# Two decoder layers with routed experts: the order of the expert blocks, the choice of experts and the causal mask are rearranged

## The chip, the cores and the metric

The kernel runs on one core of one Trainium2 chip, as one launch. The metric is the device time of one execution in microseconds. The kernel before takes 2188.45 us, the median of three timed runs (2186.95 to 2190.23). All traces show one profiled execution.

## The reference

Two layers over 1024 tokens of width 1024, all in f32. A layer is:

```python
h = h + concat(rmsnorm(SGU), rmsnorm(Conv), rmsnorm(MLA)) @ w_o     # three mixers on rmsnorm(h)
m = rmsnorm(h, ffn_norm_g);  h = h + hier_moe(m, ...)
h = h + sigmoid(rmsnorm(h) @ ple_gate_w) * rmsnorm(p @ ple_proj_w)
```

MLA is causal attention with 8 heads (`s = where(kpos <= qpos, s, -1e30)` before the softmax). What matters here is the expert part:

```python
glog = t @ wg + bg;  g_idx = argmax(glog);  g_w = softmax(glog)[g_idx]      # 4 groups
elog = (t @ we + be) restricted to the 8 experts of group g_idx
topv, topi = top_k(softmax(elog), 2);  topv = topv / sum(topv)
# each of the 2048 (token, choice) pairs goes to its expert; for an expert e and its rows xb:
hb = silu(xb @ w_gate[e]) * (xb @ w_up[e])          # w_gate, w_up: 1024 x 256, w_down: 256 x 1024
out[token] += (hb @ w_down[e]) * g_w * topv
```

Each expert's weights are 3 MB. Its rows are grouped in blocks, and a block needs the expert's weights once.

## The kernel before

Each engine has its own program, and semaphores order them. `Steps` names the steps of one chain: `X.next("name")` is what an instruction signals, `X.after(l, "name")` what another waits for. A layer runs through these stages (times of layer 1 in the profiled execution):

- **Input projection and mixers** (to about 245 us): eight tiles of 128 tokens in a loop.
- **Attention** (245 to 437 us): 8 heads of 8 query tiles, written out. For tile `j` PE computes `scores` (L1942 to L1968): one or two products of 96 rows by up to 1024 columns into PSUM, and then the product of `ident_b` and `mask_b` on the diagonal block (L1967), which adds -1e30 above the diagonal and signals the tile. VectorE takes the maximum (`row_max`, L1458), ScalarE the exponential with that as its bias (L1064), PE transposes it (L1976) and multiplies by the values (L1996). PE issues the scores of the next tile ahead of the transposes of the present one. VectorE also runs the taps of a convolution in between (L1290).
- **Output projection** (437 to 592 us): a loop over tiles. VectorE's and ScalarE's programs are real loops (`lag_loop`, L414), two tiles a turn, in which each stage `(o, fn)` works on tile `t + o`; PE's is written out (L2064). VectorE's order (L1510) is: `norm_m` of the tile before (L1262, the norm whose result goes to the experts), `norm(1)` of tile t+2 (L1253), copy of the transposes of t+1 (L1269), `conv_centre` of t+3, copy of `turn_m` (L1274), the first half of `h +=` (L1503), `conv_scale`, `conv_silu` of t+3 (L1382), the second half, `g_main` (L1508, the router's logits of tile t-1), `conv_out` of t+3 (L1387). The three convolution steps run in iterations 0 to 4 only (tiles 3 to 7; tiles 0 to 2 are done inside attention). PE's order is: first half of the projection, `turn(1)` of t+1, `conv_back`, `turn_m` of t-1, second half, `conv_turn` of t+3 (L1869, needs `conv_silu`), the logits of t-1, `pointwise`. Behind the loop comes tile 7's remainder: `norm_m`, `turn_m`, logits.
- **Router** (592 to 625 us): a chain of small VectorE steps over all tiles (L1531 to L1666), each of which waits for the one before (`link`, L1516). It chooses a group and two experts for each token (L1531 to L1559), `picked` (L1557) goes to PE for the counts (L2093, L2097), which PE issues behind `project(0)` and `project(1)` (L2082), products for the last line of the layer. Then the blocks are laid out. `owner_f`, `owner_i` (L1620, L1621) write each block's expert to `cells`; SP waits for that and loads the weights of blocks 0, 1 and 2 (L650 to L658). The one-hot products (L1630, L1631, L2119, L2122) give the lists of rows (`list_i`, L1662), for which GpSimd waits before it gathers the rows of the first three blocks (L817).
- **Experts** (625 to 957 us): an expert with a remainder of up to 64 rows gets a *small* block (64 rows) for it, all else goes to *full* blocks (128 rows). Blocks come in pairs: the small one first, on even positions, the full one behind it. `n_pairs` is the larger of the number of full blocks and half of all blocks, rounded up, and 2 x `n_pairs` blocks are run (`n_blocks`, L1639). Three buffers `slot` hold weights. For block b PE's order is: gate and up (L2160 full, L2156 small), transposes of the rows of b+1 (L2141), down of b-1 (L2181 full, L2175 small), transposes of the hidden units (L2188). SP loads gate and up of b+2 (L643, L644) when those of b-1 have been used, and down of b+2 (L648) when `down` of b-1 is finished. `block_loop` (L462) unrolls six blocks, with a guard for each step.
- **Last line of the layer** (957 to 1110 us), which starts when all blocks are stored.

## Time and profile before

| | us |
|---|---|
| timed runs, median of 3 | 2188.45 |
| the profiled execution | 2190.6 |
| its span, first to last instruction | 2188.8 |
| PE matmuls busy | 2000.5 (91%) |
| VectorE busy | 1009.4 (46%) |
| ScalarE busy | 638.8 (29%) |
| GpSimd busy | 374.5 (17%) |
| DMA moved 362 MB, mean | 165 GB/s |

The chain of work that ended last is the thread to follow: it starts at the last instruction and steps back to whatever released each one. By engine it is 76% PE, 11% DMA, 5% VectorE, 4% issue, 3% ScalarE. The DMA share lies in the two expert stages. The mean granted TensorE clock was 0.969 of full speed. In the rows, `PE` is a matmul, `PEld` a weight load, `DVE` VectorE, `ACT` ScalarE, `POOL` GpSimd, `SPq` SP's queue; a release is shown as `[idle before <-releaser]`. A matmul on f32 stands as two instructions.

### The profile page before, as it was taken

Reading aid. Unit: us, or ns where it says so; the run is one execution under the profiler, and the core shown is the slowest. Engines: PE = TensorE matmul, PEld = TensorE weight load, DVE = VectorE, ACT = ScalarE, POOL = GpSimd, SP = SyncE. Lnnn points to the kernel's source line nnn. Section 1 sums busy time; section 2 is a strip of 40 time slices with the busy share of each in tenths; the row PEclk is TensorE's granted clock in tenths of the full one; section 3 lists DMA queues with packets and bytes.
Section 4 is the critical chain, followed back from the end, with each engine's and each line's share of the span. In section 5 each row is a group of like instructions: output and inputs, shape, how many; then the busy total and the mean of one; then the engine's idle time right before and its main releaser. Section 6 shows DMA issues by size and latency. Waiting matters only on the chain.

```text
span 2188.8 us, 34749 instructions
## 1 busy us (share of the span) xinstructions
PE 2000.5 (91%) x9032; PEld 1110.8 (51%) x9032; DVE 1009.4 (46%) x2247; ACT 638.8 (29%) x1521; POOL 374.5 (17%) x542
## 2 busy tenths in 40 slices
PE   6999799899969999989979998998999699999898
PEld 3555466655535455544435554666555354445344
DVE  2489756654341111124434897566543421111253
ACT  3333355522111111131133333555221111111221
POOL 2232100021012222210022221000210122221100
PEclk9999899999979999999989998999999799999999
DMA  7011241000389999955210112410004799999422
GB/s 249 15 29 29 59 153 30 25 20 29 140 308 396 380 382 378 389 217 192 88 29 15 29 29 61 152 30 25 20 29 154 292 393 381 377 380 353 175 87 96
DMA packets 122222, 361.98 MB, mean 165 GB/s; under 512 B 18853, under 2 KB 54005, under 8 KB 105220
## 3 DMA queue, kind: packets, MB, share of 16 engines
q1 hardware_dynamic: 105028, 318.74, 40.2%
q0 software_dynamic: 14784, 33.59, 4.1%
q10 hardware_dynamic: 2304, 8.39, 0.9%
q8 instruction: 48, 0.79, 0.1%
q14 instruction: 58, 0.48, 0.1%
HBM read 319.50 MB, written 59.51 MB: 173 GB/s over the span
## 4 chain that ended last, share of the span: by engine, by line
PE 76%; DMA 11%; DVE 5%; issue 4%; ACT 3%; SPq 1%; DVEq 0%; POOL 0%; ACTq 0%; POOLq 0%
PE ps L1801 30%; DMA region_c<-in_moe_w_up_dram 8%; PE ps L2160 7%; PE ps L1964 5%; PE ps L1822 4%; PE ps L2156 4%; PE ps L1996 3%; PE ps L2181 3%; PE ps L1976 3%; PE ps L1770 3%; PE ps L2175 2%; PE ps L2141 2%; PE ps L1896 2%; DMA region_a<-in_moe_w_up_dram 2%; PE ps L2082 2%
## 5 line engine op out<-in xcount | busy, mean ns | idle before, releaser
L1801 PE MATMUL ps<-region_b,region_c 128*128 128x512 f32 x1024 | 451.5, 597 | 7.7 <-DVE region_c L1269 7.7
L1801 PEld LDWEIGHTS ps<-region_b,region_c 128*128 128x128 f32 x1024 | 192.8, 191 | 234.4 <-issue 233.9
L1801 PE MATMUL ps<-region_a,region_c 128*128 128x512 f32 x512 | 225.3, 594 | 0.0
L1680 DVE SCALAR_TENSOR_TENSOR region_a<-region_a,ps 128x128 f32<-128x128 f32 x66 | 23.4, 354 | 387.0 <-ACT region_a L1132 382.7
L2160 PE MATMUL ps<-region_c,region_a 128*128 128x512 f32 x336 | 148.8, 596 | 12.9 <-DMA region_c<-in_moe_w_up_dram 12.8
L1801 PEld LDWEIGHTS ps<-region_a,region_c 128*128 128x128 f32 x512 | 96.9, 191 | 118.0 <-issue 118.0
L1460 DVE TENSOR_REDUCE neg_max<-ps 128x1 f32<-128x128 f32 (+7 forms) x128 | 97.0, 758 | 109.8 <-PE ps L1967 109.0
L1964 PE MATMUL ps<-region_c 96*128 96x512 f32 (+3 forms) x384 | 146.9, 492 | 0.0
L1132 ACT ACTIVATE region_a<-ps 128x128 f32<-128x128 f32 x66 | 21.8, 330 | 364.7 <-PE ps L2160 243.5
L1976 PE MATMUL ps<-ident,region_a 128*128 128x128 f32 x576 | 91.1, 285 | 25.2 <-ACT region_a L1064 25.0
L2160 PEld LDWEIGHTS ps<-region_c,region_a 128*128 128x128 f32 x336 | 62.1, 190 | 92.9 <-issue 92.9
L1822 PE MATMUL ps<-region_a,region_c 128*128 128x416 f32 x256 | 96.2, 530 | 3.7 <-ACT region_c L940 3.0
L1770 PE MATMUL ps<-ident,region_c 128*128 128x128 f32 x496 | 66.7, 281 | 35.9 <-DVE region_c L1253 30.3
L1064 ACT ACTIVATE region_a<-ps,neg_max 128x128 f32<-128x128 f32 (+7 forms) x128 | 96.2, 752 | 0.1
L2156 PE MATMUL ps<-region_c,region_a 128*64 128x256 f32 x736 | 88.7, 395 | 5.4 <-DMA region_c<-in_moe_w_up_dram 4.0
L2160 PE MATMUL ps<-region_a 128*128 128x512 f32 x192 | 85.2, 596 | 6.7 <-DMA region_a<-in_moe_w_up_dram 5.2
L1770 PEld LDWEIGHTS ps<-ident,region_c 128*128 128x128 f32 x496 | 59.2, 144 | 61.8 <-DVE region_c L1253 34.1
L1996 PE MATMUL ps<-region_a,region_c 128*64 128x128 f32 x1152 | 84.0, 278 | 2.4 <-ACT region_a L1052 2.0
L1976 PEld LDWEIGHTS ps<-ident,region_a 128*128 128x128 f32 x576 | 61.5, 140 | 48.5 <-ACT region_a L1064 35.6
L1996 PEld LDWEIGHTS ps<-region_a,region_c 128*64 128x64 f32 x1152 | 68.9, 136 | 26.4 <-issue 26.4
L1964 PEld LDWEIGHTS ps<-region_c 96*128 96x128 f32 x384 | 65.2, 196 | 31.2 <-issue 30.8
L1049 ACT COPY region_a<-ps 128x512 f32<-128x512 f32 (+3 forms) x128 | 64.8, 506 | 55.8 <-PE ps L1976 55.8
(351 smaller groups left out, 3065.4 us busy)
## 6 DMA issues: line engine op xcount, KB each, us to landing
region_c<-in_moe_w_gate_dram SPq DMA_DIRECT2D x44, 1024.0 KB
region_c<-in_moe_w_up_dram SPq DMA_DIRECT2D x44, 1024.0 KB
region_c<-in_moe_w_down_dram SPq DMA_DIRECT2D x44, 1024.0 KB
region_a<-in_moe_w_gate_dram SPq DMA_DIRECT2D x22, 1024.0 KB
region_a<-in_moe_w_up_dram SPq DMA_DIRECT2D x22, 1024.0 KB
region_a<-in_moe_w_down_dram SPq DMA_DIRECT2D x22, 1024.0 KB
region_c<-choice_outputs SPq DMA_DIRECT2D x32, 512.0 KB, 4.4
qk_heads<-gains SPq DMA_DIRECT2D x32, 384.0 KB, 3.9
```

Source lines behind the costliest of these rows:

```text
L1049: ins = nc.scalar.copy(prob_t[j % 2][:, 0:w], bank(4, 0, w * P).rearrange("p (k q) -> p k q", q=P))
L1064: nc.scalar.activation(prob[j % 2][:, 0:n], banks(2 * (j % 2))[:, 0:n], ACT.Exp, bias=neg_max[:, j % 2:j % 2 + 1], accum_out=denom[:, j:j ...
L1460: v.tensor_reduce(neg_max[:, j % 2:j % 2 + 1], banks(2 * (j % 2))[:, 0:(j + 1) * P], AX.X, ALU.max, negate=True).then_inc(*X_max.next(f"ma ...
L1770: ins = T(bank(b + k // 4, P * (k % 4), P * (k % 4) + P), src[:, P * k:P * k + P], ident[:, :])
L1801: ins = mm(dst, lhsT[:, k, :], w[:, k, a:b], start=(k == 0), stop=(k == KD - 1))
L1822: ins = mm(bank(4, 0, MLA_IN), aT_mix[u][:, k, :], w_in[:, k, 1024:IN], start=(k == 0), stop=(k == KD - 1))
L1964: mm(bank(b + c // 512, 0, w), q, k_ring[u][0:QK, c:c + w], start=True, stop=not last, skip_group_check=True)
L1976: ins = T(bank(4 + k // 4, P * (k % 4), P * (k % 4) + P), prob[j % 2][:, P * k:P * k + P], ident[:, :])
L1996: ins = mm(ps[a:a + HEAD, 6, 0:P], vals[:, k, head, :], prob_t[c][:, k, :], start=(k == 0), stop=(k == j + c), tile_position=(0, a), skip_ ...
L2156: ins = mm(ps[a:a + HALF, 2, 0:F].rearrange("p (a f) -> p a f", a=2), xT[:, k, 0:HALF], pair[:, :, P * c:P * c + P], start=(k == 0), stop= ...
L2160: ins = mm(bank(2).rearrange("p (a f) -> p a f", a=2), xT[:, k, :], w_gu[s][:, :, k, :], start=(k == 0), stop=(k == KD - 1))
L2181: ins = mm(bank(4 + half), hid_t[:, k, :], w_dn[s][:, k, 512 * half:512 * half + 512], start=(k == 0), stop=(k == 1))
```

## The change

Four edits, none of which changes what is computed:

1. **Mask.** For tiles `j >= MASKED = 3` PE's mask product is left out, and `row_max` adds `mask_b` to the diagonal block in PSUM before it takes the maximum. VectorE waits for its own addition.
2. **Choice by tile.** `choose(t)` is a new last-but-one stage of VectorE's loop in the output projection, behind `g_main` and ahead of `conv_out`. It has 15 steps, each waiting for the one before, and takes the place of the router's 23 steps over all tiles. The exponential of the groups on ScalarE, `g_sum` and `g_w` move behind.
3. **Owners early.** `owner_f` and the two halves of `owner_i` are moved from behind `fields` to behind `key`.
4. **Full first.** In each pair the full block comes first, the small one second (all the places with `True` and `False` swap, and the lists are written to the other parity). If there are fewer small blocks than pairs, the last position is dropped (`no_last` is -1 or 0). As the numbers of full and small blocks can now differ, `cells` has separate counts of finished ones.

```diff
@@ VectorE, attention
                 def row_max(hh, j):
                     v.wait_ge(*S_pe.after(hh, f"s{j}"))
+                    if j >= MASKED:
+                        own = banks(2 * (j % 2))[:, j * P:(j + 1) * P]
+                        v.tensor_tensor(own, own, mask_b[:, :], ALU.add).then_inc(*X_mask.next(f"mask{j}"))
+                        v.wait_ge(*X_mask.after(hh, f"mask{j}"))
@@ PE, scores
+                    if j >= MASKED:
+                        ins.then_inc(*S_pe.next(f"s{j}"))
+                        return
@@ VectorE, output projection
+                def choose(t, u, i):
+                    g = TILES * l + t
+
+                    def link(ins, name):
+                        ins.then_inc(*CH_vec.next(name))
+                        v.wait_ge(*CH_vec.after(g, name))
+
+                    v.wait_ge(*G_vec.after(g))
+                    g_max, g_first, m1, i1, m2, i2 = (span(sm(k), t, 1) for k in (0, 3, 4, 5, 6, 7))
+                    gl_, el = lg[:, t, 0:NG], lg[:, t, NG:NG + NE]
+                    link(v.tensor_reduce(g_max, gl_, AX.X, ALU.max), "g_max")
+                    link(v.tensor_scalar(g_gap[:, t, :], gl_, g_max, None, ALU.subtract), "g_diff")
+                    link(v.scalar_tensor_tensor(g_cand, gl_, g_max, order[:, 0:NG], ALU.is_lt, ALU.add), "g_cand")
+                    link(v.tensor_reduce(g_first, g_cand, AX.X, ALU.min), "g_first")
+                    link(v.tensor_scalar(g_far, order[:, 0:NG], g_first, -BIG, ALU.not_equal, ALU.mult), "g_far")
+                    link(v.tensor_tensor(e_in.rearrange("p (g e) -> p g e", g=NG), el.rearrange("p (g e) -> p g e", g=NG),
+                                         g_far.unsqueeze(2).to_broadcast([P, NG, EPG]), ALU.add), "e_in")
+
+                    def largest(src, top, where, hot, n):
+                        link(v.tensor_reduce(top, src, AX.X, ALU.max), f"m{n}")
+                        link(v.scalar_tensor_tensor(cand, src, top, order[:, :], ALU.is_lt, ALU.add), f"cand{n}")
+                        link(v.tensor_reduce(where, cand, AX.X, ALU.min), f"i{n}")
+                        v.tensor_scalar(hot, order[:, :], where, None, ALU.is_equal).then_inc(*CH_vec.next(f"hot{n}"))
+
+                    largest(e_in, m1, i1, hot1[:, t, :], 1)
+                    v.wait_ge(*CH_vec.after(g, "hot1"))
+                    link(v.scalar_tensor_tensor(e_rest, hot1[:, t, :], -2 * BIG, e_in, ALU.mult, ALU.add), "rest")
+                    largest(e_rest, m2, i2, hot2[:, t, :], 2)
-                             (3, late(conv_scale)), (3, late(conv_silu)), (0, w_main(1)), (-1, g_main), (3, late(conv_out))])
+                             (3, late(conv_scale)), (3, late(conv_silu)), (0, w_main(1)), (-1, g_main), (-1, choose), (3, late(conv_out))])
@@ VectorE, router (23 steps g_max .. hot2 over all tiles removed)
+                v.wait_ge(*K_pe.after(l, "owners"))
+                link(v.tensor_copy(owner, ps[0:1, 6, 256:256 + POS]), "owner_f")
+                at_place = cells[0:1, 0:POS].rearrange("p (r a) -> p a r", a=2)
+                link(v.tensor_scalar(at_place[:, 0], owner[:, NE:POS], NE - 1, None, ALU.bitwise_and), "owner_full")
+                link(v.tensor_scalar(at_place[:, 1], owner[:, 0:NE], NE - 1, None, ALU.bitwise_and), "owner_i")
...
-                link(v.tensor_scalar(total, n_pairs[0:1], 2.0, None, ALU.mult), "n_blocks")
+                link(v.tensor_scalar(no_last, n_half[0:1], n_pairs[0:1], 1.0, ALU.is_ge, ALU.subtract), "no_last")
+                link(v.scalar_tensor_tensor(total, n_pairs[0:1], 2.0, no_last, ALU.mult, ALU.add), "n_blocks")
...
+                link(v.tensor_tensor(run[:, 4:5], run[:, 4:5], n_pairs[0:1], ALU.add), "run_pairs")
+                small_now = last_rows[0:1, 210:211]
+                link(v.tensor_tensor(small_now, no_last, n_pairs[0:1], ALU.add), "small_now")
+                link(v.tensor_tensor(run[:, 5:6], run[:, 5:6], small_now, ALU.add), "run_small")
@@ PE, experts (the same swap on ScalarE, VectorE and GpSimd)
-                turn_x(prev, 0, 0, True)
-                gate_up(prev, 0, 0, True)
-                turn_x(prev + 1, 1, 0, False)
-                turn_h(prev, True)
+                turn_x(prev, 0, 0, False)
+                gate_up(prev, 0, 0, False)
+                turn_x(prev + 1, 1, 0, True)
+                turn_h(prev, False)
```

## Rows read from the trace of the kernel before

**Rows 1.** Chain that ended last, one mask product in attention: start, us, what.
```profile
359.96 0.06 PE ps L1967
```
**Rows 2.** Windows: length, busy of each engine, granted clock, DMA share, GB/s; both expert stages.
```profile
620.00:940.00 320.00, 297.50 (x1547) 160.23 (x1548) 61.79 (x154) 52.44 (x132) 79.94 (x130) 0.97 1.00 383
1713.00:2022.00 309.00, 281.30 (x1457) 150.38 (x1458) 57.85 (x144) 48.84 (x122) 75.06 (x122) 0.97 0.99 378
```
**Rows 3.** Timeline, tile 6 of a head: start, us, engine, line, op.
```profile
360.06 1.09 DVE L1460 TENSOR_REDUCE neg_max<-ps 128x1 f32<-128x896 f32 x1 [0.28 <-PE ps L1967]
361.25 0.29 DVE L1468 TENSOR_TENSOR region_a<-ps,rden 128x128 f32<-128x128 f32 x1
361.52 1.02 ACT L1064 ACTIVATE region_a<-ps,neg_max 128x896 f32<-128x896 f32 x1
```
**Rows 4.** Two lines alone: duration in ns, min, median, max; first and last start.
```profile
L1322 DVE TENSOR_SCALAR st_c<-st_c x16: 169/170/171, 347.7 to 1614.5; 128x4 f32<-128x4 f32 x16
...
L1407 DVE SCALAR_TENSOR_TENSOR region_b<-region_b,r_c,k_gain x16: 243/246/248, 31.7 to 1302.5; 128x32 f32<-128x32 f32 x16
```
**Rows 5.** Timeline of VectorE, output projection of layer 1.
```profile
512.26 0.20 DVE L1508 TENSOR_TENSOR region_a<-ps,router_b 128x36 f32 x1 [1.25 <-PE ps L1801]
513.19 0.42 DVE L1387 SCALAR_TENSOR_TENSOR region_a<-ps,vecs 128x256 f32 x1 [0.73 <-PE ps L1876]
...
517.93 1.14 DVE L1253 SCALAR_TENSOR_TENSOR region_c<-region_a,rstd,gains 128x256 f32<-128x256 f32 x2
520.82 0.69 DVE L1269 COPY region_c<-ps 128x512 f32<-128x512 f32 x1 [1.74 <-PE ps L1770]
...
526.84 0.43 DVE L1382 SCALAR_TENSOR_TENSOR region_b<-region_b 128x256 f32<-128x256 f32 x1 [0.48 <-ACT region_b L971]
...
566.23 0.20 DVE L1508 TENSOR_TENSOR region_a<-ps,router_b 128x36 f32 x1 [1.02 <-PE ps L1801]
...
582.63 0.20 DVE L1508 TENSOR_TENSOR region_a<-ps,router_b 128x36 f32 x1 [1.03 <-PE ps L1801]
```
**Rows 6.** Timeline of VectorE, router of layer 1: linked steps with fixed addresses.
```profile
609.10 0.42 DVE L1602 SCALAR_TENSOR_TENSOR region_c<-vecs,ps 128x256 f32<-128x256 f32 x1
...
612.87 0.21 DVE L1620 CAST region_c<-ps 1x64 int32<-1x64 f32 x1
613.11 0.18 DVE L1621 TENSOR_SCALAR cells<-region_c 1x64 int32<-1x64 int32 x1
```
**Rows 7.** Timeline of VectorE, a later loop: linked steps that address by tile.
```profile
1015.82 1.28 DVE L1713 SCALAR_TENSOR_TENSOR h<-region_c,moe_weights,h 128x1024 f32 x1
1017.25 1.28 DVE L1716 SCALAR_TENSOR_TENSOR h<-region_c,moe_weights,h 128x1024 f32 x1
```
**Rows 8.** Chain that ended last, output projection and start of the router.
```profile
528.74 0.22 PE ps L1869 x2
...
573.01 0.87 PE ps L1770 x8
...
584.05 2.06 DVE region_c L1262
...
592.52 9.35 PE ps L2082 x16
```
**Rows 9.** Chain that ended last, first gather and first blocks of layer 1.
```profile
625.35 7.84 DMA region_a<-moe_inputs,block_tokens
...
642.12 7.11 PE ps L2160 x16
...
649.86 1.88 PE ps L2175 x16
...
652.11 3.61 PE ps L2156 x32
```
**Rows 10.** Timeline of SP's queue: two loads of `w_down`, 14 pairs apart.
```profile
660.20 0.38 SPq L648 DMA_DIRECT2D region_a<-in_moe_w_down_dram  x1
...
924.47 0.38 SPq L648 DMA_DIRECT2D region_c<-in_moe_w_down_dram  x1
```

More of the change, by code:

```diff
@@ L359, in build @@
         S_pe, O_pe = steps("s_pe", [f"s{j}" for j in tiles]), steps("o_pe", [f"o{m}" for m in couples])
+        X_mask = steps("x_mask", [f"mask{j}" for j in tiles if j >= MASKED])
         B_pe = steps("b_pe", [f"back{m}" for m in couples])
@@ L677, in _ @@
                 for u in range(2):
-                    sp.wait_ge(y_stored[u], (half + pairs) * 16)
+                    sp.wait_ge(y_stored[u], (done[u] + (pairs if u else smalls)) * 16)
                 settle(sp, passed)
@@ L823, in _ @@
                 gp.sem_inc(M_idx.sem, 3)
[L824 removed]
+                prev, n, done = counters(gp, l, passed, halves=True)
                 def gather(b, s, m, small):
@@ L1119, in _ @@
                     embedded(t)
-                prev, n, half = counters(act, l, passed, halves=True)
+                prev, n, done = counters(act, l, passed, halves=True)
                 def x_lo(m, small):
```

132 lines of the change are left out of this document (57 added, 75 removed).

## Prediction

> **What bounds the kernel now.** I read the chain that ended last first, then the windows by stage, then the timelines around each place that the diff touches. The attention stage and the output-projection loop are paced by PE: in the chain its matmuls follow one another, the mask products among them [rows 1], and short holes stand only at the end of a head or of the loop. The expert stage is paced by the transfers: over its 320 us in layer 1 the DMA share is 1.00 at 383 GB/s while PE is busy for 297.5 us, and layer 2 is alike [rows 2]. Between the two lies a stretch of small VectorE steps (the router), with PE's projection of `p` beside its first half. So I ask of each edit: does it shorten what PE does in the first two stages, does it move the start or the volume of the transfers in the third, and does an added VectorE step stay under cover.
>
> **Masks by VectorE.** From tile 3 on, five of a head's eight score tiles lose the product of identity and mask: 40 a layer. Each is 0.06 us of the chain [rows 1], so 2.4 us a layer leave PE. VectorE gets an addition of 128x128 in PSUM, 0.29 us by the scaling of the same size, L1468 [rows 3], plus a link, 0.32 us; the score tile is reported 0.06 us sooner, so the maximum ends 0.26 us later. The tightest cover that I found is tile 6: the maximum ends at 361.15 and ScalarE takes the exponential at 361.52 [rows 3], a slack of 0.37 us, the same in seven of eight heads; tiles 3, 4, 5 and 7 have more in the same view. PE's transposes of tile 6 come after further work of its own. Taken: -2.4 a layer, **-4.8 us** in all; if the cover fails the gain is gone (0).
>
> **Experts chosen by tile.** 23 linked steps over all tiles leave the router; 15 steps per tile enter VectorE's loop, behind the logits and ahead of `conv_out`, 120 a layer. Their cost by the nearest rows: a step of 4 columns takes 0.17, one of 36 columns 0.20, one of 32 columns with a scalar from memory 0.25 [rows 4, 5]. Two narrow reductions at 0.17, three narrow steps with such a scalar at 0.22 (an estimate, 0.17 and the 0.05 between the last two), six plain ones of 32 columns at 0.20, four with a scalar at 0.25: 3.2 us. Each waits for the one before. Where addresses are fixed the pause between linked steps is 0.03 us: L1620 ends at 613.08, L1621 starts at 613.11 [rows 6]. In a loop over tiles they are computed, and then it is 0.15: L1713 ends at 1017.10, L1716 starts at 1017.25 [rows 7]. All 15 address by tile, so a choice takes 3.2 + 15 x 0.15 = **5.4 us** in the loop, and 3.2 + 0.5 = 3.7 for tile 7, which stands behind the loop.
>
> What is queued behind it on VectorE? Three places.
> (a) Iterations with convolution work. Logits end at 512.46; `conv_out` starts at 513.19; from it the norm of tile t+2 follows through ScalarE and GpSimd and ends at 519.07; the copy L1269 starts at 520.82, when PE has its transposes; then come centring, scaling and the gate L1382, which ends at 527.27 [rows 5]; PE wants that at 528.74 [rows 8]. Free time on this way: 0.73 + 1.75 + 1.47 = 3.95 us. A choice of 5.4 overruns it by 1.4. PE then issues the next logits 1.4 later, so it repeats. Choices begin at iteration 1, convolution ends at iteration 4, and a choice is felt one iteration on: iterations 2, 3 and 4, 3 x 1.4 = 4.2 us.
> (b) Tile 6's norm: logits end at 566.43 [rows 5], the choice at 571.8, and L1262 takes 2.06 [rows 8], to 573.9; PE wants it at 573.01 [rows 8]: +0.9. One tile earlier it just fits.
> (c) Tile 7's norm: logits of tile 6 end at 582.83 [rows 5], L1262 starts at 584.05 and is on the chain, PE waiting [rows 8]. Behind a choice it starts at 588.2: +4.2.
> Sum 9.3 a layer, **+18.6 us**.
>
> What comes back? The router reaches the count of the experts sooner on VectorE, but the count is a product that PE issues behind `project(0)` and `project(1)`: 9.35 us from 592.52, to 601.87 [rows 8]. The old choice ends just before that. Taken: 0, because PE's order is unchanged and tile 7's choice, 3.7 us, is covered by the same projection.
>
> Here the Trainium skill speaks against the change. The trace shows 0.17 us for 4 columns and 0.20 for 36 [rows 4, 5], so nearly all of such a step is fixed. The page "VectorE: DVE Perf Modes", section "The TRN2 errata", says that VectorE pays a fixed latency for each instruction and that many small tiles pay it each; its formula (N + 151)/0.96 ns gives 0.16 and 0.19 for 4 and 32 columns. By the formula alone, which has neither computed addresses nor scalars from memory, the 15 steps would be an estimated 2.7 us, under every cover of (a) and (b); with the measured pauses the two readings lie 0.5 us apart.
>
> **Owners read early.** The two reads, L1620 and L1621, end at 613.29 and will stand where L1602 started, at 609.10 [rows 6], as three steps of about 0.21: they end at 609.7, so SP issues the first weights 3.6 us sooner. On the way to the lists this adds 0.2; behind the one-hot products seven small steps more (two of them moved, `g_sum` and `g_w`) at about 0.2 and the divided list make 1.5 us. The lists for GpSimd so come 1.7 us later, the weights 3.6 us sooner.
>
> **Full block first.** The first gather carries a full block's rows and is issued 1.7 us later; the small one took 7.84 from issue to landing [rows 9]. The first gate-and-up product becomes the full kind, 7.11 instead of 3.61 [rows 9]; buffer 0, and with it the fourth load, is free only behind it. That is 1.7 + 3.5 later, and more if the bigger gather takes longer, against transfers 3.6 ahead. As the stage is bound by transfers, the early weights help only if the queue doesn't run dry in front of the fourth load. Bounds per layer: -3.6 (nothing lost) and +3.3 (the whole delay reaches the end); taken 0, between them. At the end of layer 2 a small block is now last: the pause for the hidden units is covered and the last store is half as large: -1.
>
> The Trainium skill has a rule with another result. The gather's 7.84 us stand behind 6 MB of weights in the trace [rows 9]. The page "DMA: Bandwidth & Descriptors", section "Queues, rings and completion order", says that each DMA engine takes packets from its rings in turn. By that the gather would not wait for the weights, and these would not be slowed by it for long. What it would mean here is rival 2.
>
> **An empty last small block left out.** The routing follows from the reference and its inputs alone: in layer 1, 17 full and 16 small blocks are needed, so 17 pairs were run, with one empty small block; the new count is 33 instead of 34. In layer 2 it is 14 and 18, 16 pairs, nothing is left out. A block is half of a pair: 264.27 us between two loads that lie 14 pairs apart [rows 10], 18.88 a pair, 9.4 a block, if transfers bind to the end. If PE does, its products alone are 3.61 + 1.88 = 5.5 us [rows 9]. The last pairs of layer 1 run on PE without a wait for weights, so I take 7, between the two: **-7 us**. Other additions (the table `order`, more counters to load) lie at the start or behind waits for gathers: 0.
>
> **Sum.** -4.8 + 18.6 - 7 - 1 = +5.8 us. The profiled execution took 2190.6 us (span 2188.8), 2.1 above the median 2188.45 of the timed runs. Added to the profile's own time that is 2196.4, and against the median **2194.2 us**, +0.27%.
>
> **Rivals.**
> 1. The choice is cheap: the pause is 0.03 also with computed addresses, a choice takes 3.7, and (a) and (b) vanish; (c) is 2.4 a layer. Sum -4.8 + 4.8 - 8 = -8: 2180.5, faster. It decides below a choice of 4.0 us. For it: linked steps in the same loop with fixed addresses pause little; against it the pause of 0.15 [rows 7].
> 2. The transfers' early start is worth its full 3.6 a layer (the rule of rings in turn, or a queue never dry), and leaving out saves 9.4: 5.8 - 7.2 - 2.4 = -3.8: 2184.7, the same within the bound. For it the share of 1.00 [rows 2]; against it the slow first gather [rows 9].
> 3. The mask additions push the exponentials, and the full first block delays the stage: the 4.8 is lost and 3.3 a layer added: 5.8 + 4.8 + 6.6: 2205.6. For it the slack of only 0.37 at tile 6 [rows 3].
> 4. The last block isn't left out, or runs empty all the same: +7, 2201.
>
> **How the numbers follow.** Forecast 0.50 (own range 2188 to 2200), rival 1 0.14, rival 2 0.16, rival 3 0.17, rival 4 0.03. A difference of 0.2%, 4.4 us, is about what a measurement can tell here: the bounds are 2184.1 and 2192.8. Of the forecast two thirds lie above 2192.8, and rivals 3 and 4 too: slower 0.52. Same 0.28: a third of the forecast and most of rival 2. Faster 0.20: rival 1 and the rest. The range takes in rival 1's edge and part of rival 3's: 2181 to 2203.
>
> **What would show it.** In the loop of the output projection: 15 short VectorE steps behind each logits line, 5.4 us together, tiles 1 to 4 at 20.0 instead of 18.6 us, and tile 7's norm 4.2 us later behind its logits. In attention: heads 0.3 us shorter, exponentials not later. In the router: `ranks` still released by the projection. The first weights issued 5.3 us further ahead of the first gather than before; whether the early transfers pay is seen in the DMA share ahead of the fourth load: a hole there means that they don't. Layer 1: 33 loads of each weight, layer 2: 32. A choice under 4 us, or a convolution gate that PE doesn't wait for, makes the prediction wrong.

## The result, and the profile after

The changed kernel takes 2209.05 us, the median of 6 runs (2206.8 to 2215.2), against 2189.63 for the kernel before (6 runs, 2187.0 to 2192.8): 1.0095 times as long, 95% interval 1.0079 to 1.0112. That is 19.4 us more by the medians, 20.8 by the ratio. The forecast was 5.8 more, 2194.2 us, with a range of 2181 to 2203. The profiled execution of after took 2215.2 us (span 2213.4), the slowest of its six, so the spans lie 24.6 us apart, 5 more than the medians.

I cut both profiled executions at the same events (first score products, first `w_o` product, `project(0)` behind the loop, `project` behind the blocks):

| stretch, us | before | after | difference |
|---|---|---|---|
| start to first scores (same code) | 264.6 | 266.5 | +1.9 |
| attention, layer 1 and layer 2 | 174.15, 174.4 | 173.0, 172.85 | -1.2, -1.5 |
| output projection, layer 1 and 2 | 153.8, 152.5 | 162.8, 162.9 | +9.0, +10.5 |
| router and blocks, layer 1 and 2 | 368.4, 359.1 | 369.6, 364.8 | +1.2, +5.7 |
| blocks' end to the next scores, and to the end | 397.8, 144.2 | 397.4, 143.6 | -0.4, -0.6 |

So the loop of the output projection took most of it, and the expert part, where a gain of 8 was expected (7 for the block left out, 1 at the end of layer 2), took 6.9 more instead. Of the 10.5 in layer 2, 1.7 is no work of the change: the first `w_o` product took 8.83 us in this execution and 7.13 in that of before, as it does in unchanged code too (last section). The chain of after that ended last shows both (start, us, what):

```profile
558.51 2.11 DVE region_c L1267
...
575.94 2.07 DVE region_c L1267
...
593.25 2.07 DVE region_c L1267
...
602.27 9.66 PE ps L2108 x16
...
637.02 9.94 DMA region_a<-moe_inputs,block_tokens
...
649.85 9.77 PE ps L2186 x16
...
972.00 9.05 PE ps L2108 x16
```

`norm_m` (L1267) now stands on it for three tiles, each with PE waiting, where before only tile 7's did [rows 8]. The first gather is issued 34.75 us behind `project(0)` instead of 32.83 and takes 9.94 instead of 7.84 [rows 8, 9], and the first product of the blocks is the full one, 9.77 us long. Why `norm_m` is late stands in VectorE's timeline of after, from tile 6's logits (first line) through the choice (15 steps, L1536 to L1548) to tile 7's norm:

```profile
587.96 0.20 DVE L1517 TENSOR_TENSOR region_a<-ps,router_b 128x36 f32 x1 [1.03 <-PE ps L1823]
588.29 0.16 DVE L1536 TENSOR_REDUCE region_a<-region_a  x1
588.62 0.23 DVE L1537 TENSOR_SCALAR region_a<-region_a  x1 [0.17 <-DVE region_a L1536]
588.88 0.22 DVE L1538 SCALAR_TENSOR_TENSOR region_a<-region_a,order 128x4 f32<-128x4 f32 x1
...
592.66 0.24 DVE L1548 TENSOR_SCALAR region_a<-order,region_a 128x32 f32 x1
593.25 2.06 DVE L1267 SCALAR_TENSOR_TENSOR region_c<-h,rstd_m,gains 128x1024 f32<-128x1024 f32 x1 [0.34 <-issue]
```

From the end of the logits to `norm_m` it is 5.09 us; before it was 1.22 [rows 5, 8]. In the blocks, the windows of after behind the first gather (length; busy of PE, PEld, DVE, ACT and POOL; granted clock, DMA share, GB/s) show DMA engines that stand idle:

```profile
642.00:647.00 5.00, 0.00 (x0) 0.00 (x0) 0.00 (x0) 0.00 (x0) 0.28 (x1) 0.50 1.04 360
647.00:652.00 5.00, 4.12 (x11) 2.72 (x12) 0.69 (x1) 0.59 (x1) 1.25 (x2) 0.50 0.99 370
652.00:657.00 5.00, 5.00 (x9) 1.98 (x9) 0.00 (x0) 0.00 (x0) 0.00 (x0) 0.68 0.52 123
657.00:662.00 5.00, 3.68 (x17) 1.59 (x15) 1.18 (x3) 1.13 (x3) 0.61 (x2) 1.00 0.07 12
662.00:667.00 5.00, 4.89 (x41) 3.76 (x42) 0.73 (x3) 0.86 (x2) 0.80 (x2) 1.00 0.96 400
667.00:672.00 5.00, 5.00 (x14) 2.24 (x13) 1.23 (x2) 0.85 (x2) 0.00 (x0) 1.00 0.34 84
```

The first two have full shares, and a granted clock of 0.50 behind PE's idle time: the first block starts at that clock. The shares of the other four leave out 0.48 + 0.93 + 0.04 + 0.66 = 2.11 windows, 10.5 us; 1.41 windows, 7 us, are one hole, and the 0.66 follows later. Before there was no such hole in the stretch that answers to it (kernel before, same columns):

```profile
642.00:647.00 5.00, 4.88 (x12) 2.28 (x13) 0.00 (x0) 0.00 (x0) 1.17 (x2) 1.00 1.03 407
647.00:652.00 5.00, 5.00 (x32) 2.50 (x30) 1.39 (x4) 1.13 (x3) 0.00 (x0) 1.00 1.04 338
652.00:657.00 5.00, 5.00 (x42) 3.35 (x42) 1.02 (x4) 1.24 (x3) 2.49 (x4) 1.00 0.98 383
```

The hole of 7 us ends when SP issues the fourth block's gate weights (the fourth load), which waits for the first block's gate and up products. SP's queue, after and then before:

```profile
660.48 0.35 SPq L647 DMA_DIRECT2D region_c<-in_moe_w_gate_dram  x1
```
```profile
641.02 0.34 SPq L643 DMA_DIRECT2D region_c<-in_moe_w_gate_dram  x1
```

Counted from `project(0)` that is 58.2 us after, 48.5 before.

### The profile page after: what moved, and what is told of

It reads as the page before. It is cut to its first block, busy times and chain, and to the rows that moved or that the text cites. A ratio compares the mean times of both kernels' runs of the same rounds, so it can differ in the third digit from the quotient of the medians.

```text
span 2213.4 us, 35185 instructions
## 1 busy us (share of the span) xinstructions
PE 1998.4 (90%) x8895; PEld 1102.6 (50%) x8895; DVE 1068.2 (48%) x2538; ACT 637.4 (29%) x1517; POOL 370.9 (17%) x538
## 3 DMA queue, kind: packets, MB, share of 16 engines
q10 hardware_dynamic: 2304, 8.39, 1.0%
## 4 chain that ended last, share of the span: by engine, by line
PE 67%; DMA 12%; DVE 8%; issue 5%; ACT 4%; SPq 1%; POOL 1%; DVEq 1%; ACTq 0%; POOLq 0%
PE ps L1823 25%; DMA region_c<-in_moe_w_up_dram 7%; PE ps L2186 7%; PE ps L1986 4%; PE ps L1844 4%; PE ps L2002 3%; PE ps L2022 3%; DMA region_a<-in_moe_w_up_dram 3%; PE ps L2207 3%; PE ps L2182 3%; PE ps L1792 2%; PE ps L1918 2%; PE ps L2108 2%; PE ps L2201 2%; PE ps L2167 2%
## 5 line engine op out<-in xcount | busy, mean ns | idle before, releaser
L1702 DVE SCALAR_TENSOR_TENSOR region_a<-region_a,ps 128x256 f32<-128x256 f32 (+1 forms) x65 | 23.1, 356 | 386.7 <-ACT region_a L1136 386.7
L2186 PE MATMUL ps<-region_c,region_a 128*128 128x512 f32 x368 | 169.4, 615 | 13.0 <-DMA region_c<-in_moe_w_up_dram 11.3
L1136 ACT ACTIVATE region_a<-ps 128x256 f32<-128x256 f32 (+1 forms) x65 | 21.5, 331 | 364.6 <-PE ps L2186 251.7
L2186 PEld LDWEIGHTS ps<-region_c,region_a 128*128 128x128 f32 x368 | 70.6, 197 | 104.1 <-issue 104.1
L1792 PE MATMUL ps<-ident,region_c 128*128 128x128 f32 x496 | 67.9, 283 | 46.8 <-DVE region_c L1258 30.7
L2207 PE MATMUL ps<-region_c,region_a 128*128 128x512 f32 x184 | 82.9, 593 | 0.6 <-ACT region_a L1141 0.6
L2167 PE MATMUL ps<-ident,region_a 128*128 128x128 f32 (+1 forms) x520 | 60.5, 259 | 24.1 <-DMA region_a<-moe_inputs,block_tokens 24.1
```

Source lines behind the costliest of these rows:

```text
L1792: ins = T(bank(b + k // 4, P * (k % 4), P * (k % 4) + P), src[:, P * k:P * k + P], ident[:, :])
L2167: ins = T(bank(k // 4, w * (k % 4), w * (k % 4) + w), x_blk[s][0:w, P * k:P * k + P], ident[0:w, 0:w])
L2186: ins = mm(bank(2).rearrange("p (a f) -> p a f", a=2), xT[:, k, :], w_gu[s][:, :, k, :], start=(k == 0), stop=(k == KD - 1))
L2207: ins = mm(bank(4 + half), hid_t[:, k, :], w_dn[s][:, k, 512 * half:512 * half + 512], start=(k == 0), stop=(k == 1))
```

## The parts, one at a time

Each part was put on the kernel before by itself. The kernel before was run between the others in every comparison; its medians were 2190.4 to 2191.9.

### The masks alone

```diff
+        v.tensor_tensor(own, own, mask_b[:, :], ALU.add)      # tiles 3 to 7, ahead of the maximum
-        mm(..., ident_b[:, :], mask_b[:, :], start=False, stop=True)
```

> The kernel before with the masks of turns 3 to 7 added by VectorE, and nothing else. The two profiles place 1.1 us (layer 1) and 1.7 us (layer 2) of gain between the last projection ahead of attention and the first W_o product. Theory A (that was the masks, the rest of each profile's difference is not theirs): 2.8 us less than the kernel before. Theory B (the forecast on record: 2.4 us a layer): 4.8 us less, and the two profiles hid part of it. Theory C (attention gains nothing, the difference of the profiles is the granted clock): within 1 us of the kernel before.

Measured: 2190.59 us against 2191.85, ratio 0.9992 (0.9981 to 1.0002). In its trace attention takes 172.98 and 172.88 us from the first score product to the first `w_o` product; in the six traces without this edit it takes 174.1 to 174.4. So the gain is 1.2 to 1.5 us a layer, 2.7 in all, and the time, 1.8 less by the ratio, can't tell that from nothing. In the profiled execution the first `w_o` product took 8.83 us in both layers, in that of the kernel before 8.83 and 7.13, which hides 1.7 us of it there. Theory A holds for the stage, and the whole is as near to C.

### The choice by tile alone

```diff
-     (-1, g_main), (3, late(conv_out))
+     (-1, g_main), (-1, choose), (3, late(conv_out))        # and the router's 23 steps left out
```

> The kernel before with the choice of experts by tile inside the W_o loop, and nothing else: small block first, owners read late, masks by TensorE. Theory A (each 5.0 to 5.4 us choice stands in front of the next tile's norm_m, for which TensorE waits, and the shorter router gains nothing because the ranks wait behind the projections of tiles 0 and 1): the W_o loop is 9 us longer in each layer, the router within 0.5 us of before, in all 17 to 19 us more than the kernel before. Theory B (the extra time of the changed kernel comes from what the choice triggers later, in the router and in the block stage): the W_o loop is longer, but the whole is 20 us or more above the kernel before. Theory C (a good part of the choice hides): under 12 us more.

Measured: 2211.16 us, ratio 1.0087 (1.0074 to 1.0100), 19 us more. Theory A. The loop takes 164.3 and 161.5 us; router and blocks 368.7 and 361.1, so 0.3 and 2.0 more than before. The distances between the starts of successive logits products, read from PE's timelines of layer 1, show where it goes:

| from tile to tile, us | 0-1 | 1-2 | 2-3 | 3-4 | 4-5 | 5-6 | 6-7 | sum |
|---|---|---|---|---|---|---|---|---|
| before | 18.57 | 18.57 | 18.57 | 18.14 | 17.27 | 16.39 | 7.81 | 115.3 |
| after | 19.72 | 19.15 | 19.71 | 18.14 | 18.00 | 17.40 | 12.24 | 124.4 |
| choice alone | 20.04 | 20.25 | 19.74 | 18.14 | 18.04 | 17.39 | 12.26 | 125.9 |
| one choice moved | 20.19 | 19.25 | 19.94 | 19.82 | 18.25 | 17.50 | 8.39 | 123.3 |
| choice in two halves | 18.57 | 18.58 | 18.57 | 18.13 | 17.27 | 16.40 | 8.37 | 115.9 |

The 7.81 of before is no fair base for the last column: there the eight transposes of tile 7's norm took 1.41 us. In the four other runs without a choice in the loop (masks, both with the full block first, owners early) they took 1.97 us in layer 1, and the distance is 8.36 to 8.38. So of the 4.4 us behind tile 6's choice 3.9 are the choice's.

### One choice moved, its work kept

```diff
+                def choose_early(t, u, i):                   # in choose's place in the loop
+                    if isinstance(t, int):                   # tile 7, behind the loop
+                        choose(TILES - 2, 0, 0)
+                        choose(TILES - 1, 1, 0)
+                        return
+                    guarded(v, i < PAIRS - 1 if u == 0 else True, go)   # go: choose(t, u, i)
```

> The run with the choice by tile alone, but tile 6's choice is moved behind the last logits, next to tile 7's: the same 16 choices with the same instructions, one of them no longer in front of tile 7's norm_m. Theory A (a choice costs by where it stands: seven places of the loop cost 1.1, 0.6, 1.1, 0, 0.7, 1.0 and 4.4 us by the distances of the logits in the changed kernel's trace): last distance 7.8 us instead of 12.3, the others unchanged, ranks no later since they wait for the projections of tiles 0 and 1; 8 to 9 us less than with all choices in the loop, about 2202 (11 us above the kernel before). Theory B (what is moved comes back behind the loop): ranks 4 us later after the first projection, no gain. Theory C (the choice's work costs, not its place): under 3 us of gain.

Measured: 2205.27 us, ratio 1.0074 (1.0060 to 1.0089). VectorE's timeline of this run:

```profile
586.69 0.20 DVE L1509 TENSOR_TENSOR region_a<-ps,router_b 128x36 f32 x1 [1.03 <-PE ps L1816]
588.11 2.07 DVE L1263 SCALAR_TENSOR_TENSOR region_c<-h,rstd_m,gains 128x1024 f32<-128x1024 f32 x1 [1.23 <-POOL rstd_m L754]
```

Tile 7's norm starts 1.22 us behind the logits again and the last distance falls from 12.26 to 8.39 (7.50 in layer 2, from 12.27); the others stay within 0.25 us but for two in layer 1, one 1.0 shorter and one, the 19.82, 1.7 longer. The ranks start 9.67 us behind `project(0)`, as in the changed kernel (9.59): the choice that was moved is covered there. The loop bears out theory A in its place: 4.2 and 4.0 us less. The profiled spans lie 8.7 apart. The medians are only 5.9 apart, and by the ratios it is 2.8, with intervals that overlap, which is theory C's figure. How much of the 8 reaches the end this run doesn't settle.

### Full block first, with and without the last block

```diff
-    turn_x(prev, 0, 0, True)     # small
+    turn_x(prev, 0, 0, False)    # full; the other places and the lists alike
+    link(v.tensor_scalar(no_last, n_half[0:1], n_pairs[0:1], 1.0, ALU.is_ge, ALU.subtract), "no_last")
```

> The kernel before with the full block first and the empty last small block left out (33 instead of 34 blocks in layer 1, 32 in layer 2), owners still read late, choice and masks as before. Theory A (a full first block takes 9.8 us instead of 5.1 us for its gate and up products at the low granted clock, the fourth block's weights are issued that much later and the DMA engines stand idle for it; nine more small router steps; a longer way out where the last block is small): layer 1 about 1.5 us less, layer 2 about 6 us more, 4 to 5 us more in all. Theory B (the forecast on record: order costs nothing, the block left out gives 7 us): 7 us less. In the trace A wants a hole in DMA of about 10 us behind the first block, B none.

Measured: 2196.05 us, ratio 1.0023 (1.0015 to 1.0032). Theory A. By its trace layer 1 is as before (368.4 us of router and blocks) and layer 2 takes 6.2 more. The hole is there, half as deep as in the changed kernel, 0.33 + 0.29 + 0.39 = 1.01 windows:

```profile
645.00:650.00 5.00, 3.73 (x33) 2.73 (x34) 1.18 (x3) 1.13 (x3) 1.41 (x3) 1.00 0.67 244
650.00:655.00 5.00, 5.00 (x28) 2.96 (x24) 1.26 (x3) 1.45 (x3) 0.00 (x0) 1.00 0.71 293
655.00:660.00 5.00, 5.00 (x13) 2.15 (x12) 0.69 (x1) 0.27 (x1) 1.54 (x3) 1.00 0.61 218
```

The other kernel keeps the empty block:

```diff
-    link(v.tensor_scalar(no_last, n_half[0:1], n_pairs[0:1], 1.0, ALU.is_ge, ALU.subtract), "no_last")
+    link(v.tensor_scalar(no_last, n_half[0:1], 0.0, None, ALU.mult), "no_last")
```

> As the run before, but the empty last small block is kept (34 blocks in layer 1). The difference of the two is the price of one block. Theory A (the block loop of layer 1 is bound by the weights' stream, 9.4 us a block): 9 to 10 us more than with the block left out, so about 14 us more than the kernel before. Theory B (the forecast on record, 7 us for the block): 7 us more than with the block left out. Theory C (the empty block hides in the stream's backlog): under 3 us more.

Measured: 2202.16 us, ratio 1.0046 (1.0030 to 1.0062). The block left out is worth 6.1 us by the medians and 5.0 by the ratios; in the traces layer 1 takes 317.9 us from the fourth load to `project` with it and 311.6 without it, 6.3. That is nearest to B's 7, and not A's 9.4. A reason that fits, though no run tried it: without the block the last to wait for its weights is a full one, whose products take 7.11 us instead of a small one's 3.67, which gives 3.4 of the 9.4 back.

The order itself costs 10 us in the time of both layers, and 6.1 and 7.7, so 13.8, in the traces' stretches of router and blocks. From the kernel before to this one the fourth load moves by 8.1 us in layer 1 and 6.8 in layer 2, counted from `project(0)`: first gather issued 1.9 and 1.2 later, landed another 1.6 and 1.0 later, and from there to the load 4.7 and 4.6 more, for the full block's transposes and products. The first products alone take 8.63 and 9.82 us instead of the small block's 5.12 and 6.38, 3.5 and 3.4 more: both kinds run at the low clock there.

### Owners early

```diff
     link(v.scalar_tensor_tensor(keys[:, 3], keys[:, 2], 512.0, keys[:, 1], ALU.mult, ALU.add), "key")
+    v.wait_ge(*K_pe.after(l, "owners"))                       # moved up from behind "fields"
+    link(v.tensor_copy(owner, ps[0:1, 6, 256:256 + POS]), "owner_f")
```

> The kernel before with the owners of the blocks read early (small block first as before), and nothing else. Theory A (there are three buffers for weights, and the fourth load waits for the first block's gate and up products; so the loads issued 3 us sooner only end sooner, and the stream stands still for it later): first weights issued 3.4 us sooner after the first projection in each layer, the fourth load no sooner, within 1.5 us of the kernel before. Theory B (rival 2 of the forecast, the stream runs ahead): up to 3.6 us less a layer, 5 to 7 us in all. Theory C: the three steps read from TensorE's result stand in front of the lists now, first gather 0.2 us later, nothing else.

Measured: 2185.10 us, ratio 0.9977 (0.9969 to 0.9986), 5 us less. That speaks for B, and yet the trace is A's: first weights 18.8 us behind `project(0)` instead of 21.9, fourth load at 49.0 and 49.0 instead of 48.5 and 49.85, router and blocks 368.6 and 358.7 us instead of 368.4 and 359.1. Only the first two loads come sooner; the third, which waits for the stores of the projection, is issued at 37.4 and 36.3 us, before at 37.2 and 36.9.

The counterpart undoes it in the changed kernel:

> The changed kernel with the owners read late again, as before the change. Theory A (behind a full first block the early loads only wait for the fourth load, which the first block sets): within 1.5 us of the changed kernel. Theory B (reading early is worth 5 us here too, as it was beside the small first block): 4 to 6 us more than the changed kernel.

Measured: 2214.61 us, ratio 1.0110 (1.0092 to 1.0127), by the ratios 3.3 us above the changed kernel, by the medians 5.6, the intervals overlapping. It leans to B. But in layer 1 the DMA engines stand idle less, from where their share falls:

```profile
650.00:655.00 5.00, 5.00 (x19) 2.24 (x17) 0.00 (x0) 0.38 (x1) 0.00 (x0) 0.99 0.71 201
655.00:660.00 5.00, 3.57 (x34) 2.65 (x34) 1.18 (x3) 0.74 (x2) 1.41 (x3) 1.00 0.69 249
660.00:665.00 5.00, 5.00 (x24) 2.67 (x21) 1.27 (x3) 1.45 (x3) 0.00 (x0) 1.00 0.57 233
665.00:670.00 5.00, 5.00 (x14) 2.31 (x13) 0.69 (x1) 0.27 (x1) 2.09 (x3) 1.00 0.75 246
```

That leaves out 1.28 windows where the changed kernel leaves out 2.11, although the fourth load comes at nearly the same place, 57.6 us against 58.2. There the loads that were issued sooner were finished sooner, and the engines waited longer. The trace has the longer time in layer 2: fourth load at 57.6 instead of 54.9, router and blocks 369.2 instead of 364.8; in layer 1 it is 0.6 the other way.

## What sets the block stage

The first load that has to wait for a buffer is the fourth. If the time from there on is fixed, what delays it is paid in full. That was tested with TensorE products that nobody reads, put between the router and the wait for the first gather: they should raise the granted clock, and hold the first block back if there are too many.

```diff
+                for _ in range(15):
+                    mm(bank(5), ident[:, :], h[:, 0, 0:512], start=True, stop=True)
                 turn_x(prev, 0, 0, False)
```

> The changed kernel with 15 more TensorE products, of which nobody reads the result, ahead of its wait for the first gather. Theory A (the full first block costs because it runs at the low granted clock, and the fourth block's weights wait for it): clock 1.00 at the first block, its gate and up products 7 us instead of 9.8, the fourth load 3 us sooner in each layer, 4 to 6 us less than the changed kernel, near 2204. Theory B (the block stage is set by the weights' stream, whatever the first block does): within 1 us of the changed kernel, 2209. Theory C (the added products run past the gather's landing): slower than the changed kernel.

Measured: 2221.57 us, ratio 1.0138 (1.0121 to 1.0155), 12.5 us above the changed kernel: theory C, because a product took 1.04 us where I had reckoned with half. PE's timeline, and SP's queue:

```profile
639.18 15.63 PE L2218 MATMUL ps<-h,ident 128*128 128x512 f32 x30 [6.24 <-issue]
654.65 1.04 PE L2167 MATMUL ps<-ident,region_a 128*128 128x128 f32 x8
```
```profile
664.54 0.34 SPq L647 DMA_DIRECT2D region_c<-in_moe_w_gate_dram  x1
```

In layer 1 the first block starts 8 us late and runs at the high clock, 7.11 instead of 9.77. The miss is good evidence for the rule: the fourth load comes 4.6 us (layer 1) and 7.4 us (layer 2) later than in the changed kernel, 12.0 in all, router and blocks take 11.9 longer, and the time is 12.5 longer by the medians, 9.4 by the ratios. The same with 13 products on the version with halved choice (next section), small block first:

> The new version with halved choice, with 13 added products ahead of the wait for the first gather. Here the small block is first and the DMA engines have no hole behind it. Theory A (the fourth load is early enough, the stream has no hole to close): first block's products 3.6 us instead of 5 to 6.4, whole within 1.5 us of the version without them. Theory B (the start of the first block counts wherever it is): 3 to 5 us less.

Measured: 2194.65 us, 11.5 above its own base of 2183.19, 12.0 by the ratios. Neither theory: the products took 3.67 us as expected, but the added ones ran about 8 us past the landing. The fourth load comes 5.8 and 5.5 us later, 11.3 in all, and router and blocks take 9.7 longer. Six products on the changed kernel:

> The changed kernel with 6 added TensorE products, whose result nobody reads, ahead of the wait for the first gather (15 of them took 15.6 us at about 1.04 us each and ran 8 us past the landing; 6 should end at about the landing). Theory A (the end follows the issue of the fourth block's weights one for one, and the full first block at the low granted clock is what delays it): first gate and up products 7.1 us, fourth load about 3 us sooner in layer 1 and 1.5 to 2 us in layer 2, 4 to 6 us less than the changed kernel (2209). Theory B (with 15 products the time was lost by the first block's own lateness, and an earlier fourth load gives nothing): within 1.5 us of the changed kernel.

Measured: 2208.65 us, ratio 1.0083 (1.0067 to 1.0099), against 1.0095 for the changed kernel. The first products take 7.10 us as expected, but the added ones overrun the landing by about 0.6 us in layer 1 and 3 in layer 2, so the fourth load moves by only 3.0 and 0.3 us. 3.3 us sooner and 2.6 less by the ratios, 0.4 by the medians: it fits, and by its intervals proves nothing.

From the fourth load to `project` behind the blocks, in all 16 traces: layer 1 318.4 to 321.2 us with the small block first, 317.9 with the full one first and 34 blocks, 310.9 to 312.0 with 33; layer 2 308.5 to 311.6 in either order. The fourth load itself lies between 46 and 63 us behind `project(0)`. So the rule holds in the stage to about 3 us. In whole times it holds only to about 5: from the kernel before to the full block first the load comes 14.9 later in all and the time is 10 longer, and with the owners early it doesn't move and the time is 5 shorter.

## A version that is faster than both

The choice costs by its place, and the router is held by the projections that PE issues ahead of the ranks. So, on the kernel before and with the masks on VectorE: tiles 0 to 3 are chosen in one pass between the two additions to `h` of tile 6, where VectorE idles for 5.7 us, tiles 4 to 7 behind the loop; PE issues the ranks behind `project(0)` and the two halves of `project(1)` in its pauses.

```diff
-     (0, w_main(0)), (3, late(conv_scale)), ...
+     (0, w_main(0)), (0, first_half, 0), (3, late(conv_scale)), ...   # guarded: i > PAIRS - 2
+                choose(HALF_T)                                         # behind the loop
                 project(0)
-                project(1)
                 ... ranks
+                project(1, (0,))
                 ... starts
+                project(1, (1,))
```

> A new version on the kernel before: masks by VectorE; the choice of experts in two halves, tiles 0 to 3 in one pass between the two h additions of tile 6 in the W_o loop (VectorE is idle for 5.7 us there), tiles 4 to 7 behind the loop; the ranks on TensorE between the projections of tiles 0 and 1, and tile 1's projection in two halves in TensorE's pauses behind the ranks and the starts. Theory A (what costs is not the choice's work in the loop but that it stands in front of norm_m; and the router can be shortened only where the ranks don't wait behind projections): W_o loop as before within 0.7 us, the first gather 3.5 to 4 us sooner after the loop in each layer, with the masks 8 to 9 us less than the kernel before. Theory B (VectorE's work in the loop costs wherever it stands): the W_o loop 4 to 5 us longer, the gain is gone. Theory C (an earlier router only makes the weights' stream wait elsewhere): the router shorter, the whole only 1 to 2 us less.

Measured: 2183.19 us against 2190.81, ratio 0.9961 (0.9948 to 0.9975), 7.6 and 8.5 us less. Theory A, although the gather comes 3.0 and 2.6 us sooner and not 3.5 to 4. The loop's distances are those of the runs without a choice in it (table above): this half costs nothing there. It isn't the same code as the choice by tile: 19 steps over four tiles, with fixed addresses. Its timeline in the router, VectorE's last step of the choice and PE's ranks, with `project(1)` behind them:

```profile
598.75 0.42 DVE L1575 TENSOR_TENSOR region_a<-region_a 128x256 bf16<-128x256 f32 x1
```
```profile
599.32 0.34 PE L2118 MATMUL ps<-ones_b,region_a 128*32 128x1 bf16 x8 [0.36 <-DVE region_a L1575]
600.51 0.68 PE L2107 MATMUL ps<-region_b,region_c 128*128 128x512 f32 x1
```

The ranks start 5.7 us behind `project(0)` instead of 9.3, the first gather is issued at 29.8 and 29.7 us instead of 32.8 and 32.35, the fourth load at 46.3 and 46.5 instead of 48.5 and 49.85. The masks, the halved choice and the place of the ranks were not run apart here.

With the owners early as well:

> The version with halved choice, with the owners read early as well. Theory A (reading early gives what the place of the fourth load shows in the profile, 1.4 us in all; the rest of the 5 us by which the run with owners early alone was faster is not its own): 1 to 2 us less than the version with halved choice. Theory B (5 us are its own, by the third block's weights or the two first ones ending sooner): 4 to 6 us less.

Measured: 2179.88 us against 2190.43, ratio 0.9956 (0.9939 to 0.9972), the fastest, 10.5 us below the kernel before and 29 below the changed one. Beside the version without it the ratio falls by 0.0005, 1.1 us, the medians by 3.3: A rather than B, though the trace has no earlier fourth load (46.6 and 47.4 us against 46.3 and 46.5). Six added products on that:

> The same, with 6 added products ahead of the wait for the first gather. Theory A (time follows the fourth load): the small first block's products 3.6 us instead of 5 to 6, fourth load 1.5 to 2.5 us sooner in each layer, 3 to 5 us less than without them, the fastest of all versions. Theory B (with the small block first the stream has no hole to close): within 1 us of the version without them.

Measured: 2179.99 us, ratio 0.9960 (0.9945 to 0.9974). The first products take 3.67 us instead of 5.8 and 6.0, but the added ones end 2 us or more behind the landing, and the fourth load stays at 46.8 in both layers (46.6 and 47.4 without them). No gain, as B had it, but not for B's reason. And the changed kernel's order of blocks on that version:

> The whole change with the choice mended: masks by VectorE, owners early, full block first, empty last small block left out, and the choice in two halves with the ranks between the projections of tiles 0 and 1. Theory A (the parts add up: full block first with the block left out costs 4 us on the kernel before, and early owners give nothing behind a full first block): 4 to 9 us more than the version with small block first, about 24 us less than the changed kernel, 2184 to 2188. Theory B (with an earlier router the order of the blocks costs nothing): as fast as the small block first, or faster by the block left out (up to 6 us).

Measured: 2188.26 us, ratio 0.9990 (0.9979 to 1.0002), 8.4 us above the small block first. Theory A: fourth load at 54.05 and 53.3 us. The 8.4 (7.4 by the ratios) is the order with the block left out; on the kernel before these two together cost 4 to 5. So the order costs at least as much behind a shorter router.

## Why the prediction was wrong, step by step

- **Masks, -4.8 forecast.** Mis-sized: the stage gave -2.7. VectorE's maximum ends later, and the exponential at tile 6 follows it with 0.09 us of slack instead of 0.37 [rows 3], so the cover held; but a head became 0.15 to 0.2 us shorter, not 0.3. Why not 0.3 was not tried.
- **Choice, +18.6.** Right, in size and for its three reasons: measured 19 alone. In layer 1 (a) was +1.15, +0.6 and +1.1 instead of 3 x 1.4; (b) +1.0, and another +0.7 one tile earlier, which I had let fit; (c) 3.9 instead of 4.2, the delay of `norm_m`. The 0.56 us by which its transposes are longer than before (1.97 against 1.41) are the granted clock's, and they are there without a choice too. Sum 8.5 against 9.3. A choice took 4.6 us, not 5.4: its steps sum to 3.1 and the 14 pauses between them to 1.5, 0.11 each, not 0.15; another 0.5 lies ahead of it and behind it, and 5.1 against the free 3.95 of (a) gives the 1.15 that was measured. The VectorE formula of the Trainium skill ("VectorE: DVE Perf Modes", "The TRN2 errata"), cited in the forecast, gave an estimated 2.7 us for the 15 steps, and those measured sum to 3.1. With no pauses it would have left (a) and (b) covered, and they were not.
- **Nothing comes back from the router.** Right: the ranks still follow the projections, 9.6 us behind `project(0)`.
- **Lists 1.7 later, weights 3.6 sooner.** Right in size: gather 1.9 and 2.2 later, weights 3.3 and 3.0 sooner.
- **Full block first, 0, bounds -3.6 and +3.3.** This is the step that failed. The term stood for the order together with the early owners, and I had set the head start of the weights against the later fourth load and taken nothing. The order alone costs 5 us a layer in time. With the owners early beside it, 2.5 us a layer are left by the sum of the parts, and 4.3 if it is taken from the whole (20.8 less masks, choice and block). In the traces the block stages follow the fourth load's place, and the head start hardly moves that: on the kernel before 0.5 later and 0.8 sooner, in the changed kernel 0.6 later and 2.7 sooner. There the load comes 9.7 and 5.1 us later than before. The upper bound doesn't follow from the terms ahead of it either: 1.7 + 3.5 is 5.2, not 3.3, and the whole delay at the end would have been 5.2 a layer. Those two terms were nearly right (gather 1.9 and 1.2 later, products 3.5 and 3.4 longer with the full block first alone; the low clock, 8.6 to 10.0 us for the full kind instead of the 7.11 of [rows 9], lengthens both kinds alike). What lacked was the gather's later landing, 1.6 and 1.0, and 1.2 for the rest up to the load. The forecast named the sign to look for, a hole in the DMA share ahead of the fourth load, and it is there. Rival 3 had that mechanism, beside masks that fail. Its 2205.6 is the nearest of all to the measured time, in part by luck: the mask gain that it dropped is there in the stage, 2.7 of 4.8.
- **At the end of layer 2, -1.** Not seen. The pause ahead of the last `down` is hardly shorter (0.9 us against 1.0), and PE waits 7.2 us from its end for the first product of the next stage, 5.4 before (7.2 in all seven traces with the full block first, 5.4 to 5.7 in the nine others):

```profile
2058.93 1.95 PE ps L2201 x16
2060.88 7.22 issue
```

What it waits for the trace doesn't say. From the fourth load to the end of the blocks layer 2 takes 308.5 to 311.6 us with the full block first and 308.8 to 311.4 with the small one, so neither sign can be told.

- **Block left out, -7.** Nearly right: -5.0 to -6.3.
- **Owners early** had no term of their own, but were part of the 0 above. Measured -5 alone, -1 to -3 on the fastest version, and 3 to 6 when undone in the changed kernel. By the Trainium skill's rule that rings are served in turn ("DMA: Bandwidth & Descriptors", "Queues, rings and completion order") the gather would not wait for the weights queued before it. It takes 7.0 and 7.1 us from issue to the transposes with early owners, 8.0 and 8.55 without, but on the version with halved choice 8.4 and 8.9 against 7.9 and 8.3: these runs don't decide it.

By the ratios the parts sum to -1.8 + 19.1 + 5.0 - 5.0 = +17.3 us, and the whole is +20.8 (by the medians 19.4); with intervals of 2 us and more on each, they agree. Against the sum on record the masks lost 3, the order of the blocks with the block left out 13 (from -8 to +5), and the owners gave 5 back. **Still open:** where the 5 us of the early owners alone lie. In its profile the block stages hold 0.2 of them, and 6 lie in stretches whose code is the same: 264.6 to 262.9 us before the first scores, 397.8 to 393.4 between the layers. Part is a mixture: of 78 executions of the kernel before 17 had a mean granted clock of 0.970 or more, with a median of 2187.7 us, and the others 2191.7; with the owners early it was 8 of 12, 2184.6, and the others 2187.3. At like clock the gain is 3 to 4 us. Whether the edit or chance made the high clock more frequent no run shows.

## What to carry to other kernels

Work moved into idle time of an engine costs by what stands behind it in that engine's order: seven choices behind the logits, in front of the convolution and `norm_m`, cost 8.5 us a layer, a choice for four tiles between two additions nothing that the distances show. Where transfers bind a stage and buffers are few, find the first load that waits for a buffer and count everything ahead of it, at the granted clock of that moment; loads issued sooner in front of it only wait. And a chain shortened on one engine gains nothing until the other engine's order lets its product go ahead: the choice by tile left the ranks at 9.2 to 9.6 us behind `project(0)`, and only with the choice in halves and the ranks between the projections did they start at 5.7.

## What was not expected of the hardware

Executions of one kernel lie up to 12 us apart (the kernel before: 2183.9 to 2194.8; with the full block first: 2196.1 to 2207.7), and the traces show one source. PE's granted clock falls to 0.50 of full speed, the lower of its two levels (1.2 GHz), behind a pause, as in the windows of after at 642 us, and on which products the fall lies differs in stretches of the same code. The kernel before and the one with owners early, in windows that begin 360 us behind the first `project` after the blocks of layer 1:

```profile
1320.91:1340.91 20.00, 16.94 (x41) 8.05 (x40) 16.18 (x41) 4.79 (x10) 4.50 (x2) 0.83 0.27 69
1340.91:1360.91 20.00, 13.08 (x57) 9.50 (x56) 13.40 (x37) 5.20 (x9) 1.76 (x2) 0.68 0.16 40
```
```profile
1318.32:1338.32 20.00, 16.76 (x46) 7.84 (x46) 18.52 (x46) 4.52 (x10) 6.26 (x4) 1.00 0.19 52
1338.32:1358.32 20.00, 12.74 (x65) 8.99 (x66) 11.64 (x32) 7.12 (x18) 0.00 (x0) 0.74 0.31 80
```

The clocks are 0.83 and 0.68 in the one, 1.00 and 0.74 in the other. The first `w_o` product takes 8.83 us in some executions and 7.13 in others for the same reason, 1.7 us. The stretch between the layers took 393.4 to 394.1 us in six of the 16 traces and 396.6 to 397.8 in the ten others, with either order of the blocks in both groups. So one pair of profiles can be off by 5 us in its total, as here, and even stages cut at the same events can be compared to a microsecond only where the clock fell at the same place in both.
